# The opening of a two-block float32 kernel: order of the first loads and of the first products

## What is computed

```python
def rmsnorm(x, g):
    return x * lax.rsqrt(jnp.mean(x * x, axis=-1, keepdims=True) + 1e-6) * g

def swiglu(x, w_gate, w_up, w_down):          # 1024 -> 2816 -> 1024
    return (jax.nn.silu(x @ w_gate) * (x @ w_up)) @ w_down

x = x + 0.5 * swiglu(rmsnorm(x, ff1_norm), ff1_w_gate, ff1_w_up, ff1_w_down)   # the change is here
x = x + mixer(rmsnorm(x, mix_norm))           # gated MLP and stick-breaking attention
x = x + 0.5 * swiglu(rmsnorm(x, ff2_norm), ...)
x = rmsnorm(x, final_norm)
# second block: gated linear attention, swiglu, block-sparse attention, swiglu, each with a layer norm
```

## Time and profile before

| | us |
|---|---|
| median of 3 timed executions | 1260.61 |
| lowest, highest | 1260.3, 1261.57 |
| the profiled execution's own time | 1258.56 |
| its span | 1256.8 |
| busy in the span: PE, DVE, ACT | 1243.8, 756.4, 594.1 |

### The profile page before, as it was taken

The page is one execution under the profiler, slowest core; times in us unless marked ns, Lnnn a source line. Parts: engine busy times, 40 slices in busy tenths (PEclk is TensorE's granted clock), DMA queues, the critical chain, the costliest instruction groups (busy, mean ns, idle before and its releaser), DMA issues.

```text
span 1256.8 us, 15240 instructions
## 1 busy us (share of the span) xinstructions
PE 1243.8 (99%) x5959; PEld 1019.0 (81%) x5959; DVE 756.4 (60%) x1027; ACT 594.1 (47%) x784; POOL 41.8 (3%) x91
## 2 busy tenths in 40 slices
PE   8999999999999999999999999999999999999997
PEld 7888887887777888888887667888888887888886
DVE  5855656756676665556446568555657777555454
ACT  6543534556657453445335444344443554544440
POOL 3000002100000000000000000000000000000000
PEclk9999999999999999999999999999999999999999
DMA  8655654755445466556545355655663544764551
GB/s 285 200 185 199 232 186 131 243 172 148 142 149 196 153 199 205 196 189 215 192 110 168 114 166 187 204 195 181 218 206 134 187 148 135 234 200 156 197 185 50
DMA packets 119831, 226.03 MB, mean 180 GB/s; under 512 B 8120, under 2 KB 16320, under 8 KB 119760
## 3 DMA queue, kind: packets, MB, share of 16 engines
q1 hardware_dynamic: 117184, 216.10, 52.0%
q0 software_dynamic: 2560, 8.95, 2.7%
q10 hardware_dynamic: 16, 0.00, 0.0%
HBM read 223.98 MB, written 1.05 MB: 179 GB/s over the span
## 4 chain that ended last, share of the span: by engine, by line
PE 95%; DVE 3%; DMA 1%; issue 0%; POOL 0%; ACT 0%; SPq 0%; DVEq 0%; POOLq 0%; ACTq 0%
PE ps L475 29%; PE ps L485 29%; PE ps L480 28%; PE ps L422 4%; DVE X L1611 1%; PE ps L806 1%; PE ps L804 1%; PE ps L635 1%; DVE wl L1517 1%; PE ps L648 1%; DVE X L1617 0%; DMA bbc<-in_gmlp_ln_b_dram 0%; DMA raw<-in_ff_w_gate_dram 0%; DVE st L1602 0%; DVE X L1622 0%; DVE XTL L1559 0%
## 5 line engine op out<-in xcount | busy, mean ns | idle before, releaser
L1517 DVE TENSOR_TENSOR wl<-raw,wh 128x1024 fp32r<-128x1024 f32 x405 | 479.6, 1218 | 176.3 <-ACT wh L954 173.4
L954 ACT ACTIVATE wh<-raw 128x1024 fp32r<-128x1024 f32 x405 | 408.1, 1053 | 107.8 <-PE ps L485 34.1
L475 PE MATMUL ps<-wh,XTH 128*128 128x512 f32 (+1 forms) x1184 | 453.5, 387 | 0.0
L480 PE MATMUL ps<-wl,XTH 128*128 128x512 f32 (+1 forms) x1184 | 444.8, 379 | 0.7 <-DVE wl L1517 0.7
L485 PE MATMUL ps<-wh,XTL 128*128 128x512 f32 (+1 forms) x1184 | 346.8, 379 | 0.2 <-DVE XTL L1567 0.2
L475 PEld LDWEIGHTS ps<-wh,XTH 128*128 128x128 f32 x1184 | 223.4, 189 | 45.3 <-issue 4.4
L480 PEld LDWEIGHTS ps<-wl,XTH 128*128 128x128 f32 x1184 | 223.5, 189 | 41.0 <-DVE wl L1517 1.1
L485 PEld LDWEIGHTS ps<-wh,XTL 128*128 128x128 f32 x1184 | 216.0, 188 | 43.2 <-DVE XTL L1567 0.7
L475 PE MATMUL ps<-wh,HHf 128*128 128x512 f32 x352 | 137.8, 391 | 0.0
L480 PE MATMUL ps<-wl,HHf 128*128 128x512 f32 x352 | 137.1, 390 | 0.0
L991 ACT ACTIVATE HHf<-ps 128x512 fp32r<-128x512 f32 (+1 forms) x48 | 24.5, 560 | 178.7 <-PE ps L422 178.6
(11 more groups left out here) (279 smaller groups left out, 938.2 us busy)
## 6 DMA issues: line engine op xcount, KB each, us to landing
raw<-in_ffn_w_gu_dram SPq DMA_DIRECT2D x88, 512.0 KB, 4.6
raw<-in_w_in_dram SPq DMA_DIRECT2D x56, 512.0 KB, 3.7
raw<-in_ff_w_up_dram SPq DMA_DIRECT2D x44, 512.0 KB, 4.8
raw<-in_ff_w_down_dram SPq DMA_DIRECT2D x44, 512.0 KB, 4.7
raw<-in_ffn_w_down_dram SPq DMA_DIRECT2D x44, 512.0 KB, 4.9
raw<-in_ff_w_gate_dram SPq DMA_DIRECT2D x40, 512.0 KB, 4.1
raw<-in_gla_w_in_dram SPq DMA_DIRECT2D x24, 512.0 KB, 4.5
raw<-in_moba_w_in_dram SPq DMA_DIRECT2D x24, 512.0 KB, 4.9
```

Source lines behind the costliest of these rows:

```text
L475: e.matmul(o, lh[:, kt, rows(t)], high[:, w], start=kt == 0, stop=False)
L480: e.matmul(o, lh[:, kt, rows(t)], low[:, w], start=False, stop=False)
L954: e.activation(wh_of(j)[:, 0:m], raw[:, j % NR, 0:m], ACT.Copy).then_inc(S("wh"), 1)
L1517: e.tensor_tensor(wl_of(j)[:, 0:m], raw[:, j % NR, 0:m], wh_of(j)[:, 0:m].bitcast(F32), ALU.subtract).then_inc(S("wl"), 1)
```

## The change

Six edits, all in the opening:

1. SP issues chunk 0's second half ahead of x01.
2. PE turns x00's first two pieces into banks 7 and 6 and its last two into bank 4; x01 is no longer turned here. Four unread products of the identity follow.
3. Chunk 0 for row block 0 has a function of its own: high-high, high-low, low-high for the first k-piece, then the same for the second. One unread product stands after the first high-high.
4. x01 is turned between chunk 0 and chunk 1 of row block 0.
5. DVE writes x00's first low piece after chunk 0's first low half, its second after the second half, and then the other two. A semaphore `x_low` counts the first two; PE waits for each piece apart.
6. The small turn of g uses bank 2 instead of 7, the unread products bank 3 instead of 6, and ACT waits for `x_low` before the row sums of squares, which write bank 6.

```diff
--- before.py
+++ after.py
@@ -358,6 +358,12 @@
         def high(key):
             return S(f"hi{aux_table[key][0]}"), aux_table[key][4]
 
+        def turned_piece(key, k):
+
+            if key == ("x", 1, 0, 0) and k < 2:
+                return ps[:, 7 - k, P:2 * P]
+            return aux4(key)[:, k % 4, :]
+
         def aux4(key):
             return ps[:, aux_bank(key), :].rearrange("p (k n) -> p k n", k=4)
 
@@ -387,9 +393,9 @@
                 e.dma_start(raw[:, j, cols(h)], src[:, h, :]).then_inc(S(f"raw{j}" if h else f"raw{j}first"), 16)
 
             e.dma_start(X[:, 0, cols(0)], x[0, 0:P, cols(0)]).then_inc(S("x00"), 16)
-            load_half(0, 0)
+            for h in range(2):
+                load_half(0, h)
             e.dma_start(X[:, 0, cols(1)], x[0, 0:P, cols(1)]).then_inc(S("x01"), 16)
-            load_half(0, 1)
             for j in range(1, HALVES):
                 for h in range(2):
                     load_half(j, h)
@@ -448,16 +454,36 @@
 
             def wait_first(e, part, t, kt):
                 if t == 0 and kt < 2:
-                    if part == "h":
-                        e.wait_ge(S("x_high"), kt + 1)
-                    elif kt == 0:
-                        whole(e, "l", t, 0)
+                    e.wait_ge(S("x_high" if part == "h" else "x_low"), kt + 1)
                 else:
-                    whole(e, part, t, 0 if part == "h" and t == 0 and kt == 2 else kt)
+                    whole(e, part, t, 0 if t == 0 and kt == 2 else kt)
 
             return wait_first if stage == 1 else whole
 
+        def idle(e, n):
+
+            for _ in range(n):
+                e.matmul(ps[:, 3, 0:P], ident[:, :], ident[:, :], start=True, stop=True)
+
+        def pe_first_products(e, name, wait):
+
+            o = ps[:, bank_of(name, 0), :]
+            for kt in range(2):
+                w = cols(kt)
+                e.wait_ge(S("wh" if kt else "wh_first"), 1)
+                wait(e, "h", 0, kt)
+                e.matmul(o, XTH[:, kt, rows(0)], wh_of(0)[:, w], start=kt == 0, stop=False)
+                if kt == 0:
+                    idle(e, 1)
+                e.wait_ge(S("wl" if kt else "wl_first"), 1)
+                e.matmul(o, XTH[:, kt, rows(0)], wl_of(0)[:, w], start=False, stop=False)
+                wait(e, "l", 0, kt)
+                e.matmul(o, XTL[:, kt, rows(0)], wh_of(0)[:, w], start=False, stop=False)
+
         def pe_products(e, name, t, j, lh, ll, wait):
+            if t == 0 and j == 0:
+                pe_first_products(e, name, wait)
+                return
             b, at, end, width, kts = blocks[name]
             _, n, _, k0 = chunks[j]
             high, low = wh_of(j), wl_of(j)
@@ -513,6 +539,8 @@
         def pe_first(e, name, stage, halves):
 
             for now in pe_gemm(e, name, XTH, XTL, wait_x(stage), 4):
+                if now == (0, 1) and stage == 1:
+                    pe_turn_x(e, 1, 0, 1)
                 if now == (0, 3):
                     for t, h in halves:
                         pe_turn_x(e, stage, t, h)
@@ -914,17 +942,17 @@
                 advance(side)
 
         def pe_program(e):
-
-            def idle(n):
-                for _ in range(n):
-                    e.matmul(ps[:, 6, 0:P], ident[:, :], ident[:, :], start=True, stop=True)
-
             e.wait_ge(S("const"), 2)
-            idle(3)
+            idle(e, 3)
             e.wait_ge(S("grow"), 16)
-            e.transpose(ps[:, 7, 0:8], SC[0:8, 0, 0:P], ident[0:8, 0:8]).then_inc(S("gturn"), 1)
-            for h in range(2):
-                pe_turn_x(e, 1, 0, h)
+            e.transpose(ps[:, 2, 0:8], SC[0:8, 0, 0:P], ident[0:8, 0:8]).then_inc(S("gturn"), 1)
+            key = ("x", 1, 0, 0)
+            e.wait_ge(S("x00"), 16)
+            pe_wait_free(e, key)
+            for k in range(4):
+                ins = e.transpose(turned_piece(key, k), X[:, 0, rows(k)], ident[:, :])
+            pe_last_fill(key, ins)
+            idle(e, 4)
             pe_ffn(e, "f1", 1, [(1, 0), (1, 1)])
             pe_mixer(e)
             pe_ffn(e, "f2", 3, LAST[3])
@@ -991,7 +1019,7 @@
                 e.activation(dst, src, ACT.Copy).then_inc(high(key)[0], 1)
 
             def high_x(key, k):
-                return e.activation(XTH[:, k, rows(key[2])], aux4(key)[:, k % 4, :], ACT.Copy, scale=gcol[:, k:k + 1])
+                return e.activation(XTH[:, k, rows(key[2])], turned_piece(key, k), ACT.Copy, scale=gcol[:, k:k + 1])
 
             def split_x(stage, t, half):
                 key = ("x", stage, t, half)
@@ -1048,6 +1076,7 @@
                             while left:
                                 split_x(stage, *left.pop(0))
                             if f == "f1":
+                                e.wait_ge(S("x_low"), 2)
                                 for r in range(2):
                                     for h in range(2):
                                         squares(r, h, S("x1" if r else f"x0{h}"), 16)
@@ -1464,7 +1493,7 @@
             e.dma_start(SC[0:8, 0, 0:P], ff1_norm[0].rearrange("(k p) -> k p", p=P)).then_inc(S("grow"), 16)
             tables("silu_and_others")
             e.wait_ge(S("gturn"), 1)
-            e.activation(gcol, ps[:, 7, 0:8], ACT.Copy).then_inc(S("gcol"), 1)
+            e.activation(gcol, ps[:, 2, 0:8], ACT.Copy).then_inc(S("gcol"), 1)
             e.wait_ge(S("gcol"), 1)
             def high_half(j, h):
                 e.wait_ge(S(f"raw{j}" if h else f"raw{j}first"), 16)
@@ -1558,14 +1587,17 @@
                 e.wait_ge(*high(key))
                 e.tensor_tensor(dst, src, top.bitcast(F32), ALU.subtract).then_inc(emptied(key)[0], 1)
 
+            def low_piece(key, k):
+                t = key[2]
+                return e.scalar_tensor_tensor(XTL[:, k, rows(t)], turned_piece(key, k), gcol[:, k:k + 1],
+                                              XTH[:, k, rows(t)].bitcast(F32), ALU.mult, ALU.subtract)
+
             def low_x(stage, t, half):
                 key = ("x", stage, t, half)
                 if stage == 1:
                     e.wait_ge(*high(key))
-                    for i in range(4):
-                        k = 4 * half + i
-                        ins = e.scalar_tensor_tensor(XTL[:, k, rows(t)], aux4(key)[:, i, :], gcol[:, k:k + 1],
-                                                     XTH[:, k, rows(t)].bitcast(F32), ALU.mult, ALU.subtract)
+                    for k in range(4 * half, 4 * half + 4):
+                        ins = low_piece(key, k)
                     ins.then_inc(emptied(key)[0], 1)
                     return
                 low(key, XTL[:, hsl(half), rows(t)], aux4(key), XTH[:, hsl(half), rows(t)])
@@ -2228,7 +2260,11 @@
 
             for h in range(2):
                 low_half(0, h)
-            low_x(1, 0, 0)
+                e.wait_ge(S("x_high"), h + 1)
+                low_piece(("x", 1, 0, 0), h).then_inc(S("x_low"), 1)
+            e.wait_ge(*high(("x", 1, 0, 0)))
+            low_piece(("x", 1, 0, 0), 2)
+            low_piece(("x", 1, 0, 0), 3).then_inc(emptied(("x", 1, 0, 0))[0], 1)
             for h in range(2):
                 low_half(1, h)
             low_x(1, 0, 1)
```

## The result

| us | before | after |
|---|---|---|
| median of 20 timed executions | 1260.34 | 1258.59 |
| lowest to highest | 1258.85 to 1263.39 | 1258.08 to 1258.99 |
| the profiled execution's own time | 1258.56 | 1258.39 |

The last line of the table matters more: the two profiled executions differ by only 0.17 us. Before spreads over 4.5 us, after over 0.9. The change hardly shortened the best execution of the kernel (1258.85 and 1258.08 are the lowest); it removed the worse ones.

The account below looks back on a forecast made before the run. The prediction took PE's queue to set the end, with chunk 0's gain lost before chunk 2: no change, 0.0 us, plus 0.1 for chunk 2's half a little late, on the median 1260.61, gives 1260.7 us; range 1259.2 to 1261.9.

Parts of the forecast that it names:

- Swap: Loads at the start: chunk 0's second half lands at 6.1 us, and ACT converts it 0.7 us earlier.
- unread products: PE's opening: four inside its wait cost nothing, the fifth takes 0.45 us; by the main case the clock rises near 8.
- the new wait for x01's turn: ACT and DVE wait for x01's turn, now behind chunk 0; chunk 0's 1.2 us gain is lost before chunk 2.
- T: Time at which x01's turn is out on PE, taken near 9.3 us; chunk 2's second half is ready 3.57 later.
- DVE's wait in front of chunk 2: DVE waits for x01's pieces, so PE idles before chunk 2's high-low; the half is ready at 12.8 for T 9.25.
- chain B: DMAs, chunk 4's conversion near 13.3 us, then row block 1's first low-high load near 16.6: no slack, unchanged.
- I add its difference to the median: Start of the sum: made against the profiled execution, 1258.56 us, 2.05 below the median 1260.61, its difference added to the median.
- faster by what the clock gives: Rival: in timed runs the opening's clock may rise after 11.57 us; the change removes 1.0 to 1.2 us, 1259.6; chance 0.22.
- a wait outside the opening has changed: Sign of being wrong: the last load starts before 16.2 or after 17.4 us, or the median moves over 1.3 us.
- nothing in the rows shows: Against the rival of an early rise, then a stall lowering PE's clock (+2 us, 1262.7, chance 0.04): no such fall seen.

Follow-up runs that it names:

- E1: The changed kernel without its five unread products, all else of the change kept: median 1259.06 us, ratio 0.9999 to the kernel before.
- E2: The kernel before with only four unread products put between the turns of x00 and x01: median 1258.61 us, ratio 0.9993.
- E4: The changed kernel run again beside the others of its group: median 1258.47 us, ratio 0.9989 to the kernel before.
- E5: The kernel before with 64 long-satisfied waits (16 instructions) added on PE in the first swiglu: median 1259.46 us, ratio 0.9997.
- E6: The changed kernel with 236 more PE instructions, all long-satisfied waits, in the first swiglu: median 1259.54 us, ratio 0.9997 to the kernel before.
- E8: The changed kernel with the second norm's bias vector issued early, at 123.60 us in the trace: median 1257.66 us, ratio 0.9982 to the kernel before.
- E13: The kernel before, unchanged, profiled once more (first of four looks): own time 1262.04 us.
- E7: The kernel before with only the second norm's bias vector issued early, at 124.80 us instead of about 202: median 1258.60 us, ratio 0.9991.
- E3: The kernel before with only the loads of chunk 0's second half and x01 swapped: median 1259.79 us, ratio 1.0004.
- E9: The kernel before with 128 more PE instructions, all long-satisfied waits, in the first swiglu: median 1260.67 us, ratio 1.0004.
- E10: The changed kernel with 128 more PE instructions, all long-satisfied waits, in the first swiglu: median 1259.24 us, ratio 0.9996 to the kernel before.
- E12: The changed kernel with the second norm's bias vector loaded early, beside the changed kernel: median 1257.81 us, ratio 0.9983 to the kernel before, one execution left out.
- E15: The kernel before, unchanged, profiled once more (third of four looks): own time 1260.41 us.

## Why the prediction was wrong

**The working of the opening: right.** Swap, unread products, the new wait for x01's turn (T 9.18 against 9.25 to 9.3), DVE's wait in front of chunk 2, chain B at 16.53 against 16.6. Measured -0.17 us for the profiled pair against +0.1. The landings were off (chunk 0's half was ready by 5.79, not 6.1, and chunk 4 at 13.04, not 13.33), but moved the products behind them by only 0.1 us. Matched product by product, another 0.34 come at 35 us, where the turns of the first block's products took 1.31 us before and 1.03 after, and 0.1 is given back at the vector's landing. With the added products the high level began at 7.84, 7.06 and 6.64 us in three traces, near the 8 that was forecast; without them, in E1, at 9.75. Whether turns of x bring a rise was not tried.

**The step that failed** is the first of the change part: "I add its difference to the median". I took the profiled execution as a typical one and carried the 2.05 us between it and the median over as a constant. They are no constant: they are losses that this execution happened not to have, and the change removes most of them. Measured, the medians are 1.75 us apart where the profiled pair is 0.17 apart. By the table, the vector's issue is on average at 202.95 us in five executions of before and at 202.02 in three at the changed kernel, 0.9 us of opening (with the 0.3 at 35 us, which the kernels with added instructions, E2, E4, E5, E6 and E8, show too; its cause was not tried); the rest after it is 1056.81 against 1056.17, 0.6 us, nearly all from E13. Five and three executions, on several chips, give these shares only roughly.

**The rival "faster by what the clock gives"** had the right mechanism for that first part and nearly its size (1.0 to 1.2 us; 0.94 between E7 and E8, 0.9 in the table). I gave it 0.22, because "the profiled run's rise needs nothing of this". But its own arguments, a spread of 1.26 us and a profiled execution under all three timed ones, were evidence about the median, and the sum should have been made against that. The prediction had also named the sign of such an error: if the median moves by over 1.3 us, "then a wait outside the opening has changed".

**What was missing** is that an edit of PE's program can act 200 us later without any wait between. I looked for all cases in the opening. The added 20 instructions took a read out of the burst, and E7, which takes the load away from that place, lowers the median of the kernel before by 1.5 us. Shown: in the traces, a read in the main part of the burst goes with a landing of 6.2 to 6.7 us (E1, E3, E6, E13), and all the others landed in 5.1 to 5.6. Argued, not shown: that this makes up part of the 1.75 us. The timed executions do not follow the read's place alone: E5 takes the read out and gains nothing clear, E6 puts it in and E9 and E10 keep it out, and none of these four is told from the kernel before. Not shown either: how often before is hit; one execution in five was. Open: what E10's slow executions lost, why E9's DVE is late at 671 us, and how much of before's loss is such falls of the clock as in E13.

## What to carry to other kernels

One profiled execution is a draw. Where timed executions spread by more than the effect that is argued about, compare the profiled one with them first, and ask what the others have that it lacks. An unread product that fills a wait can be worth more than the order of the loads: E2 has nearly the whole gain with four of them, and its products are at the high level from 8.24 us, against 9.47 to 14.24 in five executions of before. And a load that something waits for, issued in a burst behind others, is worth a try in a quiet place: E7's median is 1.5 us below before's with one moved load, though in the changed kernel the same move gave only 0.24 us (E12). An instruction added to test a theory moves all later reads of instructions too, so a kernel with such additions needs its own comparison.

## What the runs showed that I had not expected

- A 16 KB read of instructions in a burst of broadcast loads went with 1.0 to 1.5 us on the landing of the load behind.
- PE's clock fell in two traces after short waits: after 1.87 us of waiting (E13) and after 0.60 us beside sixteen two-column products (E9). The length of the wait doesn't decide it. At 209 us PE waited 0.7 us (before), 1.04 us (E15), 2.02 us (E6) and 2.21 us (E1), and kept the high level each time. The prediction had written of such a fall that "nothing in the rows shows" one after a wait of under 2 us; here are E1's row at the wait, and E1's window behind it to compare with E13's:

```profile
211.67 0.50 PE L504 MATMUL ps<-wl,XTH 128*128 128x512 f32 x1 [2.21 <-DVE wl L1543]
```

```profile
211.60:215.40 3.80, 3.73 (x16) 3.12 (x17) 3.73 (x9) 0.32 (x1) 0.40 (x1) 1.00 0.66 191
```

- One of E12's 11 executions took 3210.2 us. Its products start 0.49 or 0.62 us apart from start to end, which is neither level, while the granted clock is recorded as 1.00; DVE's longest waits are for ACT, and ACT's for PE. PE's timeline of it from 30 us:

```profile
30.29 0.78 PE L501 MATMUL ps<-wh,XTH 128*128 128x512 f32 x1
30.91 0.78 PE L506 MATMUL ps<-wl,XTH 128*128 128x512 f32 x1
```

It happened once in some 280 executions and has no cause here; E12's other ten lie between 1257.35 and 1258.02.
